# Two transformer blocks on one core: totals of the normalisations spread by products, first weights behind them unsplit, modulation in steps of eleven, mLSTM's gate projection among the scores

## The chip, the cores and the metric

The kernel runs on one core of one Trainium2 chip. The metric is the time of one execution in device microseconds (us). TensorE (PE) has two clocks, 1.2 and 2.4 GHz; the profile gives the granted clock of a stretch as a share of the full one. VectorE is DVE, ScalarE is ACT, GpSimd is POOL, and SP is the engine that issues most DMAs.

## What is computed

For 256 tokens of width 1024, in float32, a first block with two layers and a second block with two layers. Cut to what matters:

```python
h = layer_norm(x)
for l in range(2):                                   # first block
    cq, ckv, kr, xp, xqk, xv, xo, i, f = split(h @ w_in[l])
    mix = concat(mla(cq, ckv, kr), multiscale_pool(xp), mlstm(xqk, xv, xo, i, f)) @ w_out[l]
    h = layer_norm(ALPHA * h + mix)                  # ln1
    f = conv_glu_ffn(h, w_up[l], w_down[l])
    h = layer_norm(ALPHA * h + f)                    # ln2
for l in range(2):                                   # second block, c a vector of 1024
    sh1, sc1, g1, sh2, sc2, g2 = split(silu(c) @ w_ada[l] + b_ada[l])      # the modulation
    h = rmsnorm(x) * (1 + sc1) + sh1                 # rms0
    u, q, k, v = split(h @ w_in_2[l])
    y = concat(conformer_conv(u), band_attention(q, k, v)) @ w_out_2[l]    # conv with a layernorm, cln
    x = x + g1 * y
    h = rmsnorm(x) * (1 + sc2) + sh2                 # rms1
    x = x + g2 * (swiglu(h) if l == 0 else moe_top2(h))                    # 8 experts, router on h
```

## The kernel before

Everything is kept transposed: a tensor of 256 tokens by 1024 is eight tiles of 128 partitions (features) by 256 tokens. Weights come from HBM in chunks of about 1 MB, in one fixed order, into a ring of four slots (`ring`); SP's queue issues chunk n when chunk n-4 has been read. Most weights are used as a sum of two reduced-precision parts: ACT writes the high part of half a chunk (`whi`, L909), DVE the rest (`wlo`, L1301), four halves in turn, and the activations are split likewise into `HH` (ACT) and `HL` (DVE). A tile of a product is then three fast products (`mm3`: high by high, high by low, low by high). Small weights (`w_uq`, `w_uk`, `w_mqk`, `w_uv`) are used raw in float32, each product in two passes. `pair` makes two output tiles of one chunk, 48 fast products; `ahead(n)` splits the next chunk while the current one is used.

A **normalisation** (class `Norm`) subtracts a pilot (the mean of tile 0) from each tile into `XC`, squares it into `SQ` (ACT), and adds tiles up; POOL makes nearly all of these additions (L1861), DVE some. `norm_total` sends the added tiles, and the last `direct` ones singly, through PE against a column of 1/1024: the totals of 256 tokens arrive as two columns of 128 partitions. DVE makes mean and variance of these (2 elements a partition), ACT the root (L930, L934), DVE the reciprocal (L1352), and a `diagonal` (L1333) that a product with ones spreads over all partitions again. Then DVE centres (L1359) and scales (L1374), ACT applies gain and bias into `hT` (L941) and makes `HH`, DVE makes `HL` (L1382), tile by tile in turns, and the next `pair` takes each tile as its `HL` is done. There are eleven: ln0, ln1 and ln2 of two layers, rms0, cln and rms1 of two layers.

The **modulation** runs beside the first block as generators on SP, DVE, ACT and PE, advanced by `next(mod)` once after each chunk of `w_in` (but not w_in,5), `w_up` and `w_down`. A group has eight steps, each with one DVE operation on a 512 KB chunk of `w_ada` (L1415), then the split of the sum (ACT `acc_hi`, DVE `acc_lo` L1419), then PE's 16 small products and DVE's last addition. A group takes ten steps; PE's products stand one step behind `acc_lo`. SP has two buffers (`side`) and issues load n when the sum n-2 is made.

**mLSTM and attention of the first block.** After w_in,0 PE makes the score products of three units (32-row and 128-row operands), the q, k and pool products (`w_mqk`), and for each of four heads `selh` and `sc`; then `pair` of w_in,5 (the output gate), then `num`. ACT evicts the pool product (L971) behind the split of w_out,0.

Of the kernel before, what the change touches and what calls it, by code (L numbers as in the profile page):

```python
# [109 lines left out]
class Norm:  # L110


    def __init__(self, name, src, kt, about, weight, eps, ready, before, q=("POOL", "POOL"), direct=1, sq="ACT"):
        self.name, self.src, self.kt, self.about, self.weight, self.eps = name, src, kt, about, weight, eps
        self.ready, self.before, self.q, self.direct, self.sq = ready, before, q, direct, sq


def build(nc, t, dense=False):

    with ExitStack() as ctx:  # L120
# [36 lines left out]
        def over(name, at, *shape):  # L157
# [28 lines left out]
        g_pad, g_norm, g_mod, g_tap = (  # L186
            Signal(sem(n)) for n in ("pads", "norm_pool", "mod_pool", "taps_pool"))
# [7 lines left out]
                   g_norm, g_mod, g_tap, r_w, r_mm, r_hi, r_act, r_vec, d_w, d_mm, d_hi, d_act, d_vec,  # L195
# [46 lines left out]
        for l in range(DEPTH):  # L242
            for c in range(1, 5):
                chunk(("w_in", l, c), t["w_in"][l, c], (8, 256), "col")
# [11 lines left out]
            for j in range(NJ):  # L256
                chunk(("w_up", l, j), t["w_up"][l, j], (8, 256), "col")
# [3 lines left out]
        for l in range(DEPTH):  # L261
            for c in (0, 1, 2, 4, 5, 3, 6, 7, 8, 9):
                chunk(("w_in2", l, c), t["w_in2"][l, c], *(((8, 256), "col") if c < 4 else ((4, 512), "k")))
            for c in range(4):
                chunk(("w_out2", l, c), t["w_out2"][l, c], (8, 256), "col")
            if l == 0:
                for j in range(NJ):
                    chunk(("ffn_gu", j), t["ffn_gu"][j], (8, 256), "col")
# [3 lines left out]
        chunk(("w_router",), t["w_router"], (8, 8), "k")  # L272
        seq = [(e_, f) for e_ in range(NE) for f in range(NFB)]
        first_moe = len(chunks)
        for n in range(len(seq) + 1):
# [4 lines left out]
            if n > 0:  # L280
                for c in range(2):
                    chunk(("down", *seq[n - 1], c), t["moe_down"][seq[n - 1][0], seq[n - 1][1], c], (2, 1024), "k")

# [39 lines left out]
        def raw_read(n):  # L323
            if chunks[n][3] is None:
# [81 lines left out]
        N["ln0"] = Norm("ln0", xT, 8, True, C("i1024"), "eps5", x_in, None, ("DVE", "POOL"))  # L406
        N["ln1", 0] = Norm(("ln1", 0), xT, 8, True, C("i1024"), "eps5", after_out(0), "ln0", direct=2)
        N["ln2", 0] = Norm(("ln2", 0), xT, 8, True, C("i1024"), "eps5", after_down(0), ("ln1", 0))
        N["ln1", 1] = Norm(("ln1", 1), xT, 8, True, C("i1024"), "eps5", after_out(1), ("ln2", 0), direct=2)
        N["ln2", 1] = Norm(("ln2", 1), xT, 8, True, C("i1024"), "eps5", after_down(1), ("ln1", 1))  # L410
# [2135 lines left out]
```

## Time and profile before

| | |
|---|---|
| median of three runs | 2382.81 us (2377.18 to 2387.42) |
| the profiled execution | 2385.06 us, its span 2383.3 us |
| mean granted TensorE clock | 0.950 |
| busy share of the span | PE 94%, weight loads 81%, DVE 75%, ACT 59%, POOL 2% |
| chain that ended last | PE 70%, DVE 16%, ACT 11%, issue 2%, DMA 1% |
| HBM read | 571.75 MB, 240 GB/s over the span |

The first block takes 0 to some 755 us, the second block up to its router 1305 us, the experts the rest. Matmuls are pipelined, so a busy PE isn't PE at its peak: how far apart the starts of products lie tells more than the busy time. A bracket behind a row tells how long the engine was idle before it and what ended that.

### The profile page before, as it was taken

Reading aid. Unit: us, or ns where it says so; the run is one execution under the profiler, and the core shown is the slowest. Engines: PE = TensorE matmul, PEld = TensorE weight load, DVE = VectorE, ACT = ScalarE, POOL = GpSimd, SP = SyncE. Lnnn points to the kernel's source line nnn. Section 1 sums busy time; section 2 is a strip of 40 time slices with the busy share of each in tenths; the row PEclk is TensorE's granted clock in tenths of the full one; section 3 lists DMA queues with packets and bytes.
Section 4 is the critical chain, followed back from the end, with each engine's and each line's share of the span. In section 5 each row is a group of like instructions: output and inputs, shape, how many; then the busy total and the mean of one; then the engine's idle time right before and its main releaser. Section 6 shows DMA issues by size and latency. Waiting matters only on the chain.

```text
span 2383.3 us, 31840 instructions
## 1 busy us (share of the span) xinstructions
PE 2234.9 (94%) x12980; PEld 1936.8 (81%) x12980; DVE 1778.8 (75%) x2281; ACT 1407.8 (59%) x1977; POOL 53.3 (2%) x87
## 2 busy tenths in 40 slices
PE   6999998989997988999888999999999999999998
PEld 6789998879997878999877777777777777777776
DVE  5667876657876845665855888888888888888887
ACT  5445544445543745443745767676777777776775
POOL 0010000010001000000000000000000000000000
PEclk9789998889998998999997999999999999999999
DMA  5436665435666414766412788898888888898985
GB/s 209 144 107 223 234 219 192 139 131 195 232 212 219 151 36 151 248 218 224 174 49 106 294 321 343 313 349 338 337 335 330 341 322 348 324 358 310 348 337 193
DMA packets 89431, 574.92 MB, mean 241 GB/s; under 512 B 10048, under 2 KB 10176, under 8 KB 31040
## 3 DMA queue, kind: packets, MB, share of 16 engines
q1 hardware_dynamic: 87984, 566.89, 64.2%
q0 software_dynamic: 288, 3.15, 0.4%
q10 hardware_dynamic: 1008, 2.79, 0.3%
q8 instruction: 104, 1.70, 0.3%
q14 instruction: 47, 0.39, 0.0%
HBM read 571.75 MB, written 1.05 MB: 240 GB/s over the span
## 4 chain that ended last, share of the span: by engine, by line
PE 70%; DVE 16%; ACT 11%; issue 2%; DMA 1%; DVEq 0%; POOL 0%; ACTq 0%; POOLq 0%
PE bank L456 36%; PE bank L1964 33%; DVE wlo L1301 8%; ACT whi L909 4%; DVE side L1415 2%; ACT arena L2084 1%; ACT hsh L2089 1%; DVE arena L1646 1%; ACT hT L941 1%; DVE XC L1374 1%; DVE XC L1316 0%; ACT arena L1134 0%; DVE HL L1382 0%; ACT midh L1123 0%; DMA side<-in_w_ada 0%
## 5 line engine op out<-in xcount | busy, mean ns | idle before, releaser
L1301 DVE TENSOR_TENSOR wlo<-ring,whi 128x1024 fp32r<-128x1024 f32 (+1 forms) x1006 | 1150.2, 1191 | 161.8 <-ACT whi L909 151.7
L909 ACT ACTIVATE whi<-ring 128x1024 fp32r<-128x1024 f32 (+1 forms) x1006 | 992.5, 1026 | 199.1 <-PE bank L1964 145.2
L456 PE MATMUL bank<-HH,whi 128*128 128x256 f32 x1648 | 489.7, 297 | 39.9 <-DVE HL L1382 23.8
L456 PE MATMUL bank<-HH,wlo 128*128 128x256 f32 x1648 | 477.9, 290 | 0.0
L456 PE MATMUL bank<-HL,whi 128*128 128x256 f32 x1648 | 477.7, 290 | 0.0
L1964 PE MATMUL bank<-whi,xgh 128*128 128x512 f32 x896 | 365.9, 408 | 8.7 <-DVE wlo L1301 0.8
L456 PEld LDWEIGHTS bank<-HH,whi 128*128 128x128 f32 x1648 | 326.4, 198 | 55.8 <-issue 29.0
L1964 PE MATMUL bank<-whi,xgl 128*128 128x512 f32 x896 | 354.5, 396 | 0.0
L1964 PE MATMUL bank<-wlo,xgh 128*128 128x512 f32 x896 | 353.9, 395 | 0.0
L456 PEld LDWEIGHTS bank<-HL,whi 128*128 128x128 f32 x1648 | 328.0, 199 | 0.3
L456 PEld LDWEIGHTS bank<-HH,wlo 128*128 128x128 f32 x1648 | 327.2, 199 | 0.0
L1964 PEld LDWEIGHTS bank<-whi,xgh 128*128 128x128 f32 x896 | 168.3, 188 | 72.1 <-DVE wlo L1301 36.7
L1964 PEld LDWEIGHTS bank<-whi,xgl 128*128 128x128 f32 x896 | 167.9, 187 | 41.0
L1964 PEld LDWEIGHTS bank<-wlo,xgh 128*128 128x128 f32 x896 | 169.0, 189 | 35.2
L1964 PE MATMUL bank<-whi,hsh 128*128 128x512 f32 x448 | 181.1, 404 | 4.8 <-DVE wlo L1301 2.4
L1964 PE MATMUL bank<-whi,hsl 128*128 128x512 f32 x448 | 177.4, 396 | 0.0
L1964 PE MATMUL bank<-wlo,hsh 128*128 128x512 f32 x448 | 176.7, 394 | 0.0
L456 PE MATMUL bank<-midh,whi 128*128 128x256 f32 x528 | 153.9, 291 | 3.9 <-DVE wlo L1301 3.9
L456 PE MATMUL bank<-midl,whi 128*128 128x256 f32 x528 | 153.0, 290 | 0.0
L456 PE MATMUL bank<-midh,wlo 128*128 128x256 f32 x528 | 152.9, 289 | 0.0
L1415 DVE SCALAR_TENSOR_TENSOR side<-side,cact 128x1024 f32<-128x1024 f32 x84 | 107.4, 1279 | 2.9 <-DMA side<-in_w_ada 2.9
L1964 PEld LDWEIGHTS bank<-whi,hsh 128*128 128x128 f32 x448 | 84.1, 188 | 30.1 <-DVE wlo L1301 9.4
(265 smaller groups left out, 2530.0 us busy)
## 6 DMA issues: line engine op xcount, KB each, us to landing
ring<-in_moe_gate SPq DMA_DIRECT2D x112, 1024.0 KB, 6.3
ring<-in_moe_up SPq DMA_DIRECT2D x112, 1024.0 KB, 5.2
ring<-in_moe_down SPq DMA_DIRECT2D x112, 1024.0 KB, 5.3
side<-in_w_ada SPq DMA_DIRECT2D x96, 512.0 KB, 4.0
ring<-in_w_up SPq DMA_DIRECT2D x44, 1024.0 KB, 4.9
ring<-in_w_in SPq DMA_DIRECT2D x32, 1024.0 KB, 5.0
ring<-in_w_down SPq DMA_DIRECT2D x32, 704.0 KB, 4.3
ring<-in_ffn_gu SPq DMA_DIRECT2D x22, 1024.0 KB, 4.9
```

The lines of the kernel that those rows point to most:

```text
L456: return pe.matmul(out, lhsT, rhs, start=start, stop=stop, skip_group_check=True)
L909: a.activation(hi, part, ACT.Copy).then_inc(*made.up(("hi", n, i)))
L941: a.activation(dst[:, k, :], XC[:, k, :], ACT.Identity, bias=bias(k), scale=gain(k)).then_inc(*a_norm.up((s.name, "dst", k)))
L1301: v.tensor_tensor(lo, part, hi.bitcast(F32), ALU.subtract).then_inc(*done.up(("lo", n, i)))
L1374: v.tensor_tensor(XC[:, k, :], src[:, k, :], bc(r[:, 0:S], len(ks)), ALU.mult).then_inc(*v_norm.up(*((s.name, "nrm", x) for x in ks)))
L1415: v.scalar_tensor_tensor(side_acc, side_in[n % 2], cact[:, k:k + 1], side_acc, ALU.mult, ALU.add).then_inc(*v_mod.up(("acc", n)))
L1646: v.scalar_tensor_tensor(gc[:, s:S], b[:, S:512 - s], W(f"w_fconv{l}", (2 - s) * NJ + j), gc[:, s:S], ALU.mult, ALU.add).then_inc(*v_ffn.u ...
L1964: return pe.matmul(out, lhsT, rhs, start=start, stop=stop, skip_group_check=True)
L2084: a.activation(SGB[n % 2], PS[2 * (n % 2)][:, :], ACT.Silu).then_inc(*r_act.up(("silu", n)))
L2089: a.activation(flat(HSH[(n - 1) % 2][:, :, :]), PS[BANK["turn", n - 1]][:, :], ACT.Copy).then_inc(*r_hi.up(("hst", n - 1)))
```

## The change

Four parts; the diff is cut to its core.

1. **Totals.** All additions are DVE's (`norm_add`). PE multiplies the added tile and the `direct` last ones (2; for cln all 4, for rms0 of layer 0 all 8) as moving operand with a 128x128 matrix of 1/128 (`i128`), in float32: the total of each token arrives in every partition, 256 wide. ACT squares the mean and takes the root on 128x256, DVE makes the variance, centres all tiles, takes the reciprocal on 128x256, and scales. The diagonals and the two products with ones are gone. ACT makes all eight tiles of `hT` first, then `HH`; DVE makes `HL` (`low_parts`) after all scaling.
2. **Unsplit weights** (`WHOLE`): w_in,1, w_up,0, w_in2,0, ffn_gu,0 and the router's are used raw against `hT` in float32 (`pair_whole`), two products a tile k. `ahead` passes over them: the chunk after is split one turn earlier. Their slot is free when PE has read them.
3. **Modulation**: eleven steps a group, PE's products two steps behind `acc_lo`; two steps after each of w_in,1 to w_in,4, w_v and w_xp.
4. **The gate projection** (w_in,5) is cut into 16 tiles (`pair_by_tiles`), two after each head of score units 1 and 2, two after each head's `sc`. It is split before the convolution on DVE and before the eviction of w_in,0 on ACT; ACT evicts the pool product ahead of the exponentials of the heads.

```diff
@@ PE
+            def norm_finish(s, pause=lambda: None):
+                made[0] = s.name
+                banks = [take(s.name, "mean", until=[(v_norm, s.name, "cen", s.kt // 2 - 1)])] if s.about else [None]
+                banks.append(take(s.name, "sums", until=[(v_norm, s.name, "var")] if s.about else [(a_norm, s.name, "dev")]))
+                lim = s.kt - s.direct
+                tiles = ([None] if lim > 0 else []) + list(range(lim, s.kt))
...
+                for k in tiles:
+                    for i in range(2):
...
+                        tm = mm(banks[i][:, 0:S], C("i128"), src, k == tiles[0], k == tiles[-1])
+            def pair_whole(key, until):
...
+                for k in range(8):
+                    pe.wait_ge(*whole_h(k))
+                    for m in range(2):
+                        tm = mm(b[:, S * m:S * m + S], w[:, k, 128 * m:128 * m + 128], hT[:, k, :], k + m == 0, k == 7)
...
-                        for _ in range(9):
+                        for _ in range(10):
...
-                pair(("w_in", l, 1), src, [(a_proj, "cqs0", l)])
-                next(mod)
+                pair_whole(("w_in", l, 1), [(a_proj, "cqs0", l)])
+                for _ in range(2):
+                    next(mod)
...
+                gate = pair_by_tiles(("w_in", l, 5), src, [(a_proj, "xo", l)])
...
+                        for _ in range(2 if u else 0):
+                            next(gate)
...
-                pair(("w_in", l, 5), src, [(a_proj, "xo", l)])
+                    for _ in range(2):
+                        next(gate)
+                next(gate, None)
@@ ACT
-                if n + 1 < first_moe and chunks[n + 1][3] is not None:
-                    split(n + 1)
+                m = n + 1 + (n + 1 in WHOLE)
+                if n not in WHOLE and m < first_moe and chunks[m][3] is not None:
+                    split(m)
...
+                split(CH["w_in", l, 5])
                 a.wait_ge(*p_w("w_in", l, 0, 1))
...
+                b = PS[BANK["pool", l]]
+                a.wait_ge(*p_mla("pool", l))
+                for m in range(2):
+                    proj(("pool", l, m), RAW[:, 4 + m, :], b[:, S * m:S * m + S], scale=W(f"s_pool{l}", m))
                 for h in range(4):
@@ DVE
+                if s.about and 0 < k < lim:
+                    norm_add(s, 0, k)
+                if 1 < k <= lim and k - 1 < lim:
+                    norm_add(s, 1, k - 1)
...
+                    for j in range(len(js)):
+                        centred(j)
+                v.wait_ge(*a_norm(s.name, "dev"))
+                v.reciprocal(RSTD[:, 0, :], RSTD[:, 0, :]).then_inc(*v_norm.up((s.name, "rstd")))
...
+                split(CH["w_in", l, 5])
                 v.wait_ge(*a_proj("xqk", l))
@@ SP
-                        yield
-                        if n > 8:
+                        for _ in range(3 if n > 8 else 1):
                             yield
...
-                return key[0] in ("w_v", "w_xp") or key[0] == "w_in" and key[2] != 1
+                if key[0] == "w_in":
+                    return (0, 0, 2, 2, 2, 1)[key[2]] if key[2] else 2
+                return 2 if key[0] in ("w_v", "w_xp") else 0
```

## Rows read from the trace of the kernel before

**Rows 1.** The page, busy us of each engine (share of the span).
```profile
PE 2234.9 (94%) x12980; PEld 1936.8 (81%) x12980; DVE 1778.8 (75%) x2281; ACT 1407.8 (59%) x1977; POOL 53.3 (2%) x87
```

**Rows 2.** Waits of PE: for whom, us in total, times, longest us.
```profile
PE bank L456 <- DVE HL L1382: 27.5, 26, 2.2
PE bank L456 <- DVE acc_lo L1419: 13.4, 5, 5.3
...
PE bank L456 <- DVE RSTD L1333: 10.6, 9, 1.7
PE bank L456 <- ACT XC L971: 7.9, 2, 4.0
PE bank L456 <- POOL RSTD L1861: 7.9, 1, 7.9
```

**Rows 3.** Stretches: length, busy PE, PEld, DVE, ACT, POOL; granted clock, DMA share, GB/s.
```profile
161.00:180.00 19.00, 14.36 (x70) 12.07 (x71) 12.35 (x25) 10.00 (x18) 0.00 (x0) 0.64 0.22 69
...
310.00:326.00 16.00, 10.71 (x61) 10.54 (x60) 7.22 (x11) 5.60 (x9) 0.00 (x0) 0.68 0.50 165
```

**Rows 4.** Timeline around ln1 of layer 0: start us, us, engine, line, operation.
```profile
157.38 2.89 DVE L1301 TENSOR_TENSOR wlo<-ring,whi 128x1024 fp32r<-128x1024 f32 x2 [1.43 <-ACT whi L909]
...
160.98 0.42 DVE L1625 SCALAR_TENSOR_TENSOR xT<-hT,bank 128x256 f32<-128x256 f32 x1
...
165.02 1.28 DVE L1359 TENSOR_TENSOR XC<-XC,bank 128x512 f32<-128x512 f32 x2
...
168.58 0.55 PE L456 MATMUL bank<-HH,whi 128*128 128x256 f32 x1 [2.15 <-DVE HL L1382]
...
180.39 0.28 PE L456 MATMUL bank<-HH,whi 128*128 128x256 f32 x1
```

**Rows 5.** Reciprocals on DVE by shape: count, busy us, mean ns, idle before.
```profile
L1352 DVE RECIPROCAL small<-small 128x2 f32<-128x2 f32 x11 | 1.8, 166 | 11.1 <-ACT small L934 7.2 <-ACT small L930 3.9
...
L1725 DVE RECIPROCAL arena<-arena 128x16 f32<-128x16 f32 x4 | 1.0, 252 | 14.9 <-ACT arena L1191 14.9
```

**Rows 6.** Timeline, raw float32 passes of 256 columns, at either clock.
```profile
71.66 5.56 PE L456 MATMUL bank<-arena,ring 128*128 128x256 f32 x25
...
99.82 3.78 PE L456 MATMUL bank<-arena,ring 128*128 128x256 f32 x8
```

**Rows 7.** Timeline of PE at rms0 of layer 0 and at the router.
```profile
767.58 0.99 PE L456 MATMUL bank<-cst,RSTD 128*128 128x1 f32 x4 [7.86 <-POOL RSTD L1861]
...
1292.10 0.35 PE L456 MATMUL bank<-whi,HH 128*128 128x8 f32 x1 [2.21 <-DVE HL L1382]
...
1304.57 3.67 PE L882 MATMUL bank<-cst,hT 128*128 128x128 f32 x16
```

**Rows 8.** Timeline from the scores of layer 0 to `num`, PE and DVE.
```profile
82.77 17.12 PE L456 MATMUL bank<-arena 128*128 128x128 f32 x48
...
105.66 0.42 DVE L1574 TENSOR_TENSOR SQ<-bank,cst 128x256 f32<-128x256 f32 x1 [3.33 <-PE bank L456]
...
116.50 1.65 PE L456 MATMUL bank<-arena 64*128 64x256 f32 x4 [3.96 <-ACT XC L971]
118.08 0.58 PE L456 MATMUL bank<-HH,whi 128*128 128x256 f32 x1
...
125.00 2.79 PE L456 MATMUL bank<-arena,SQ 128*128 128x65 f32 x24
```

**Rows 9.** Stretches within it, columns as in rows 3.
```profile
92.00:97.00 5.00, 5.00 (x11) 2.67 (x11) 4.63 (x9) 2.37 (x11) 0.00 (x0) 0.50 0.00 0
...
104.00:108.00 4.00, 4.00 (x14) 2.62 (x15) 2.31 (x7) 2.14 (x9) 0.00 (x0) 0.87 0.52 141
```

**Rows 10.** Timeline of DVE at the start of w_down of layer 0.
```profile
314.51 1.69 DVE L1301 TENSOR_TENSOR wlo<-ring,whi 128x768 fp32r<-128x768 f32 x2 [0.31 <-ACT whi L909]
316.12 1.22 DVE L1419 TENSOR_TENSOR acc_lo<-side,acc_hi 128x1024 fp32r<-128x1024 f32 x1
```

**Rows 11.** DMA issues of the first 140 us: count, KB each, median us to landing.
```profile
side<-in_w_ada SPq DMA_DIRECT2D x8, 512.0 KB, 6.0
```

More of the change, by code:

```diff
@@ L405, in build @@
         N = {}
[L406 to L410, printed above, removed]
@@ L416, in build @@
-        N["cln", 1] = Norm(("cln", 1), CA, 4, True, C("i512"), "eps6", lambda k: conv_made(1, k), ("rms0", 1), ("DVE", "DVE"))
-        N["rms1", 1] = Norm(("rms1", 1), xT, 8, False, C("i1024"), "eps6", lambda k: v_res("out2", 1, k), ("cln", 1), direct=2)
+        N["ln0"] = Norm("ln0", xT, 8, True, "eps5", x_in, None)
+        N["ln1", 0] = Norm(("ln1", 0), xT, 8, True, "eps5", after_out(0), "ln0")
+        N["ln2", 0] = Norm(("ln2", 0), xT, 8, True, "eps5", after_down(0), ("ln1", 0))
+        N["ln1", 1] = Norm(("ln1", 1), xT, 8, True, "eps5", after_out(1), ("ln2", 0))
@@ new lines, in build @@
+        N["ln2", 1] = Norm(("ln2", 1), xT, 8, True, "eps5", after_down(1), ("ln1", 1))
+        N["rms0", 0] = Norm(("rms0", 0), xT, 8, False, "eps6", lambda k: a_norm(("ln2", 1), "dst", k), ("ln2", 1), direct=8,
+                            sq="DVE")
+        N["cln", 0] = Norm(("cln", 0), CA, 4, True, "eps6", lambda k: conv_made(0, k), ("rms0", 0), direct=4)
+        N["rms1", 0] = Norm(("rms1", 0), xT, 8, False, "eps6", lambda k: v_res("out2", 0, k), ("cln", 0))
+        N["rms0", 1] = Norm(("rms0", 1), xT, 8, False, "eps6", lambda k: v_res("down2", k), ("rms1", 0))
@@ L419, in conv_made @@
+        N["cln", 1] = Norm(("cln", 1), CA, 4, True, "eps6", lambda k: conv_made(1, k), ("rms0", 1), direct=4)
+        N["rms1", 1] = Norm(("rms1", 1), xT, 8, False, "eps6", lambda k: v_res("out2", 1, k), ("cln", 1))
         def conv_made(l, m):
@@ L931, in norm_dev @@
                 else:
[L932 to L936 removed]
+                    a.wait_ge(*p_norm(s.name, "sums"))
+                    a.activation(RSTD[:, 0, :], b[:, 0:S], ACT.Sqrt, bias=C(s.eps), scale=1.0 / s.kt).then_inc(
+                        *a_norm.up((s.name, "dev")))
@@ L981, in act_program @@
                 norm_tile(N["ln0"], k)
-            split(0)
+            split(CH["w_in", 0, 2])
             norm_dev(N["ln0"])
@@ L986, in act_program @@
             for l in range(DEPTH):
-                split(CH["w_in", l, 2])
                 b = PS[BANK["w_in", l, 1]]
@@ L1046, in act_program @@
                 next(mod)
-                split(CH["w_in", l, 5])
                 a.wait_ge(*v_lstm("conv", l))
@@ L1558, in dve_program @@
                 next(mod)
-                split(CH["w_in", l, 5])
                 ends, causal = [], C("causal")
@@ L1661, in dve_program @@
                         norm_tile(N["ln2", l], k)
-                norm_finish(N["ln2", l], affine(N["ln2", l], hT, then=N["rms0", 0] if l else None))
+                norm_finish(N["ln2", l])
+                if l == 0:
+                    low_parts(N["ln2", 0])
+                else:
+                    for k in range(8):
+                        norm_tile(N["rms0", 0], k)
             def rms_modulated(which, l):
@@ L1932, in sp_program @@
                     next(mod)
-                if NSLOT <= n < first_moe and stepped(chunks[n - NSLOT][0]):
+                for _ in range(steps_behind(chunks[n - NSLOT][0]) if NSLOT <= n < first_moe else 0):
                     next(mod)
```

355 lines of the change are left out of this document (159 added, 196 removed).

## The prediction, made before the changed kernel was run

> **What bounds the kernel now.** I read the page's shares first, then who makes PE wait, then PE's clock by stretches, then the timelines of the places named there. PE is busy 94% of the span [rows 1], and behind a loaded weight the products follow at an even pitch (about 0.12 us a fast product in w_out,3 and in the pair that ends at 180.39), so time comes off only where PE waits, where its clock is down, or where it does fewer passes. The list of waits [rows 2] gives the places: `HL` in the normalisations 27.5 us, `acc_lo` 13.4, the diagonals (`RSTD`) 10.6, ACT's eviction of the pool product 7.9, POOL's additions 7.9 once. Each wait costs again behind itself: over the 19 us around ln1 PE is idle 4.6 and the granted clock is 0.64; over 16 us around an `acc_lo` wait it is idle 5.3 at 0.68 [rows 3]. Full clock is 2.4 GHz, 0.50 is 1.2 GHz. Behind the router's stage nothing changes, so all that is won stands at the router's end and stays.
>
> **Totals and unsplit weights.** From the last tile of xT at 160.98 to the first product behind the first pair at 180.39 ln1 takes 19.4 us [rows 4]: PE gets its first `HL` at 168.6, does 48 passes, most of them at half clock. The new chain, from that start a: 0.9 us to the last square, products with `i128` to a+2.0, variance a+2.5, four centrings at 0.61 apiece (the two in rows 4 took 1.28) to a+4.95, a reciprocal on 128x256, one scaling (0.42) and one tile of `hT` (0.5). The reciprocal isn't in the trace at this size. Its rows [rows 5] are 166 ns at 2 elements, 252 at 16: 6.1 ns an element, so 1.7 us at 256. The near bound is the pace of the simple operations (0.4 us), the far one that the slope grows by half (2.3). I take 1.7, the slope being the only row. That gives a+7.7 for the first tile, against a+7.6 before: the start doesn't move. What moves is the pair: 32 raw passes instead of 48. A raw pass is 5.56/25 = 0.222 us at full clock, 3.78/8 = 0.47 at half [rows 6]; 48 fast passes are 5.7 and 10.2. With about 5 us at half clock (11 passes) and 21 at full I get 9.6 us, range 8.8 to 10.5, so the pair ends at a+17.3: 2.1 gained. DVE's new additions in w_out are ten of 0.43 = 4.3 us; they lie in DVE's idle of 1.43 before each `wlo` [rows 4] for three of four chunks, and the last 1.0 is paid. ln1 gains 1.1 in each layer. By the same steps: ln0 2.6 (no additions on the path, PE starts on the weights at 22), ln2 of layer 0 1.5, rms1 of layer 0 and rms0 of layer 1 1.7 each, cln nothing (no pair behind it, its time is in the scores' shade). At rms0 of layer 0 POOL's 7.9 go [rows 7] and the column products of 3.7 behind it too; eight full products at half clock (7.4) and two longer reciprocals (3.0) come, and the diagonals' 1.5 go: 2.7. Sum 12.4.
>
> The Trainium skill ("VectorE: DVE Perf Modes", First, the fixed hardware budget) speaks against this part: the reciprocal is an iterative divide repeated eight times on the same slices. If an element then cost eight times that of an addition (0.42/256 = 1.6 ns, with its fixed part off about 1.0), an estimate by that page is some 2.2 us, and with nine such reciprocals on the path 5 us of the gain would be gone. The sum above goes by the slope of the rows.
>
> **Router.** Before, its first product starts at 1292.10 and its last pass ends at 1304.57: 48 narrow passes of 0.21 with two `HL` waits [rows 7]. Raw it is 32 passes at the same pitch, 6.9 us. The last square ends near 1287.0; total, root 0.45, reciprocal 1.7, scaling 0.45, `hT` 0.5 give a start at 1290.8 and an end at 1297.7: 6.9 gained. Both parts together 19.3.
>
> **Modulation.** With products two steps behind `acc_lo`, the five waits (13.4) should go where DVE was merely late, and with them the half clock behind them: in rows 3 10.7 us of busy PE at a mean of 0.68. Over the five I count 13.6 us lost to the clock. At 312 something stays: `wlo` and `midl` would be 2.3 of the 5.3 late even without `acc_lo` (the DVE rows around 316.1 show `wlo` behind `acc_lo`'s 1.22 [rows 10]). Saved: about 17 of 27. New cost: steps now come twice a chunk in the projections. A load of 512 KB takes 6.0 us to land [rows 11] and DVE's step 1.28, against 5.7 us for a pair, with two loads in it; so DVE falls behind by about 1 us a chunk there and the first group's products, now at w_xp of layer 0, wait some 2.8 us for `acc_lo`, plus the clock behind (1.7) and half a us of a late split: -5. SP's queue: two buffers, a load waits for the sum two before, and the ring's loads stand behind it; the ring has four slots in hand, so they aren't late by that much. DVE's steps in the gated and down stages are as before, one a chunk, and the number of steps, 122 before and 134 after, is met by the doubling. Net 12.
>
> **Gate projection among the scores.** In layer 0, T0 = 82.77 is the start of the scores, `num` starts at T0+42.2 [rows 8]. From 87 to 103 the clock is 0.50 [rows 9]: 32-row products of the scores leave it there, DVE and ACT pace them (DVE 5.0 of 5 us from 87, 4.6 of 5 from 92). The heads take 104.93 to 118.08 = 13.2 us with 3.96 of eviction wait, then the pair 6.9. After: 16 tiles of a third of a us to 0.64 each at either clock are put in; eight in the scores, eight in the heads. The eviction wait goes (pool product ahead of the exponentials), the heads become DVE-bound (0.42+0.28+0.56 and ACT between) at 2.15 to 2.3 a head, 9.2 in all, and contain eight tiles. In the scores, eight tiles at half clock are 5.1 us of PE; half of it lies in PE's waits for DVE, the rest lengthens them. The splits of w_in,5 (DVE 2.35, ACT 1.04) are now ahead of convolution and eviction, those of w_out,0 behind: 1.4 lost. Likeliest the scores stay at half clock: gain 13.2+6.9-9.2 = 10.9, less 3.5, less 1.4 = 6 a layer, 12 in two. If the added products lift the clock, the scores' 17 us shrink by some 8: 14 a layer. The bad end is near nothing, 0.3.
>
> **Sum.** 19.3 + 12 + 12 = 43 off the profiled execution of 2385.06 (span 2383.3, 1.8 outside) is 2342; that execution lies 2.3 above the median, so against the median of 2382.81 it is **2340**.
>
> **Rivals.** (a) The clock stays up through the scores in one layer or both: for it, full-array products between the 32-row ones; against it, DVE and ACT pace that stage at 4.6 to 5.0 of 5 us. One layer 2331, both 2323, and with the raw pairs lifted sooner 2318. (b) DVE or the side loads become the bound in the doubled stages: two 512 KB loads in a pair of 5.7 us, landing 6.0 plus 1.28. If each chunk is late by 1.6, twelve chunks cost 19, and with the added additions only 18 of the gain is left: 2365. For it, the 6.0 [rows 11]; against it, that the median is over the crowded first 140 us. (c) The other side: raw float32 pairs don't lift the clock. Then each of eight runs at 0.46 throughout, 14.4 instead of 9.8 (37 us), and the pair behind it starts cold (8 x 1.7 = 14): 51 lost against 43 gained, 2390. It decides from the point where a raw pair ends below 0.75 of the clock. Against it: the granted clock rose to 0.87 right behind the eight raw products from 99.82, beginning within them [rows 6, 9]. (d) The change does little of what it says because each wait is replaced by one as long (the centrings, now all ahead of the first scaling, push the tile as far as `HL` did, and w_xp takes over `acc_lo`'s 13.4): 2378.
>
> **How the numbers follow.** Likeliest case 0.45; (a) 0.30; (b) 0.16; (c) 0.04; (d) 0.05. The range holds the likeliest with its unknown costs (reciprocal ±5, the scores ±6) and reaches into (a) down to both layers with something to spare, and to (b): 2315 to 2366. About 0.5% (12 us) is what a measurement of this kernel can tell from no change. Faster by more than that are the first three but for an edge of (b): 0.90; within it (d) and that edge: 0.06; slower: 0.04.
>
> **What would show it.** RECIPROCAL 128x256 at 1.7 us on DVE; no addition on POOL; PE's first raw pass 7.7 us after the start of the last xT of ln1, then 32 passes at 0.46 falling to 0.22, end at a+17.3; `acc_lo` under 4 us in all, most of it once, at w_xp of layer 0; no wait for L971's successor before the last head, and `num` at T0+36; granted clock in the scores 0.50; the router's last pass 6.9 us after its first. Wrong would be: a raw pair at half clock to its end; a reciprocal over 2.3; idle of PE before w_v, w_xp or w_in,0 put down to `wlo`; the scores' span above 25 us with no gain in the heads.

## The result and the profile after

The changed kernel takes 2363.16 us (median of six, 2357.26 to 2370.51) against 2383.57 (six runs, 2377.18 to 2387.42): ratio 0.992, 95% interval 0.9904 to 0.9937. I had forecast 2340, a gain of 43 us; 20 came. The profiled execution of the changed kernel took 2358.97 us, its span is 2357.2. Against the profiled execution of before that is 26 us less; the 6 beside the medians' 20 are where the two executions lie among the runs of their kernels. The stages below are read from these two traces, so they add up to 26.

From the page of the changed kernel: the busy line of the engines, which stands beside [rows 1], and DVE's reciprocals at their new size, beside [rows 5] (columns as there).

```profile
PE 2218.2 (94%) x12766; PEld 1917.4 (81%) x12766; DVE 1784.1 (76%) x2276; ACT 1393.6 (59%) x1960; POOL 2.2 (0%) x17
...
L1411 DVE RECIPROCAL RSTD<-RSTD 128x256 f32<-128x256 f32 x11 | 19.2, 1748 | 9.8 <-ACT RSTD L982 9.6
```

PE is busy 16.7 us less, POOL does none of the additions. Waits of PE in the changed kernel (for whom, us in total, times, longest), beside [rows 2]:

```profile
PE bank L458 <- ACT hT L989: 39.5, 8, 6.2
PE bank L458 <- DVE wlo L1349: 16.6, 11, 2.7
...
PE bank L458 <- DVE SQ L1380: 7.6, 1, 7.6
PE bank L458 <- DVE HL L1461: 7.2, 7, 2.8
...
PE bank L458 <- DVE XC L1377: 6.0, 4, 2.0
PE bank L458 <- DVE RSTD L1369: 5.9, 1, 5.9
...
PE bank L458 <- DVE acc_lo L1446: 1.9, 1, 1.9
```

`HL` 27.5, `RSTD` 10.6 and POOL 7.9 of before are `hT` 39.5 and `SQ` 7.6 now: the normalisations still make PE wait as long, in one piece each. The wait for `SQ` is the new form of POOL's 7.9: at rms0 of layer 0 PE waits until DVE has squared the tiles. `acc_lo` fell from 13.4 to 1.9 and ACT's eviction of the pool product is gone. So the waits went much as the change says. The stages say where the time went instead. Each boundary is the start or the end of a PE product of the timeline that is named in the first column; the last column is the prediction's term.

| stage (us) | before | after | difference | forecast |
|---|---|---|---|---|
| to the end of ln0's first pair | 36.5 | 34.2 | -2.3 | -2.6 |
| projections, from there to the scores, layers 0 and 1 | 46.3, 46.3 | 54.5, 53.7 | +15.6 | +5 |
| scores to the first head | 22.2, 20.6 | 24.9, 24.9 | +7.0 | +7 |
| heads and the gate's pair | 20.1, 20.1 | 10.3, 10.3 | -19.5 | -21.8 |
| `num` and w_uv | 6.1, 6.1 | 12.6, 12.7 | +13.1 | +2.8 |
| attention to w_out's end | 29.6, 29.6 | 29.6, 29.6 | 0.0 | 0 |
| ln1, ln2, ln2 with rms0, rms1, rms0 of layer 1, cln | | | -9.3 | -9.8 |
| router | 19.3 | 12.4 | -6.9 | -6.9 |
| up and down, three times | 207.1, 205.5, 201.4 | 200.4, 198.9, 190.8 | -23.9 | -17 |
| experts and the rest | 1078.7 | 1078.8 | +0.1 | 0 |

The sum is -26.1, the difference of the two spans. Two terms failed: `num` and w_uv by 10.3, the projections by 10.6. The heads gave 2.3 less than forecast and the up and down stages 6.9 more; with about 1 us of the small terms that is the 17 between 43 and 26. One group of modulation products in each layer now stands in the projections and not in the up and down stages: some 4 of the +15.6 and of the -23.9 have only moved. Timeline of PE in the changed kernel, from the last head to w_uv, and under it the same products in the stretches (columns as in [rows 3]); [rows 8] has `num` of before:

```profile
120.77 0.69 PE L458 MATMUL bank<-xT,cst 4*128 4x256 f32 x2
...
123.97 1.80 PE L458 MATMUL bank<-arena,SQ 128*128 128x65 f32 x8
127.23 3.67 PE L458 MATMUL bank<-arena,SQ 128*128 128x65 f32 x16 [1.45 <-ACT arena L1013]
130.70 6.06 PE L458 MATMUL bank<-ring,arena 128*128 128x512 f32 x8
```

```profile
114.00:122.00 8.00, 8.00 (x41) 5.71 (x40) 4.75 (x13) 3.27 (x10) 0.00 (x0) 0.99 0.88 328
122.00:124.00 2.00, 2.00 (x10) 1.78 (x9) 0.94 (x3) 2.00 (x4) 0.00 (x0) 0.50 0.00 0
124.00:130.00 6.00, 4.55 (x22) 4.36 (x22) 2.77 (x4) 3.21 (x6) 0.00 (x0) 0.50 0.00 0
130.00:136.00 6.00, 6.00 (x12) 3.01 (x12) 2.68 (x7) 0.77 (x2) 0.00 (x0) 0.54 0.00 0
```

The heads run at 0.99 of the clock; from 122 it is 0.50 until 136. Before, 24 products of `num` took 2.79 us and eight of w_uv 3.65, both behind a pair in one piece, and the clock, which was down in the heads, was up again (kernel before, columns as above):

```profile
108.00:120.00 12.00, 8.04 (x24) 5.57 (x23) 4.34 (x10) 5.01 (x10) 0.00 (x0) 0.50 0.45 173
121.00:131.00 10.00, 10.00 (x68) 8.16 (x67) 3.45 (x10) 3.37 (x7) 0.00 (x0) 1.00 0.00 0
```

So the tail, `num` and w_uv, grew by 6.5 us in two ways: PE stands idle for 1.45 in the middle of `num`, where it never waited before, and the products themselves take 5 us longer at half clock.

### The profile page after: what moved, and what is told of

Same layout as the page of the kernel before. It is cut to its first block, busy times and chain, and to the rows that moved or that the text cites. A ratio compares the mean times of both kernels' runs of the same rounds, so it can differ in the third digit from the quotient of the medians.

```text
span 2357.2 us, 31258 instructions
## 1 busy us (share of the span) xinstructions
PE 2218.2 (94%) x12766; PEld 1917.4 (81%) x12766; DVE 1784.1 (76%) x2276; ACT 1393.6 (59%) x1960; POOL 2.2 (0%) x17
## 3 DMA queue, kind: packets, MB, share of 16 engines
q10 hardware_dynamic: 1008, 2.79, 0.3%
## 4 chain that ended last, share of the span: by engine, by line
PE 71%; DVE 15%; ACT 10%; issue 2%; DMA 1%; SPq 0%; DVEq 0%; ACTq 0%
PE bank L458 37%; PE bank L1973 34%; DVE wlo L1349 8%; ACT whi L954 4%; DVE side L1442 2%; ACT arena L2093 1%; ACT hsh L2098 1%; DVE arena L1681 1%; DVE RSTD L1411 1%; DMA ring<-in_w_in 1%; DVE XC L1399 1%; ACT arena L1181 0%; DMA side<-in_w_ada 0%; ACT midh L1170 0%; DVE XC L1377 0%
## 5 line engine op out<-in xcount | busy, mean ns | idle before, releaser
L1349 DVE TENSOR_TENSOR wlo<-ring,whi 128x1024 fp32r<-128x1024 f32 (+1 forms) x990 | 1128.5, 1187 | 116.2 <-ACT whi L954 106.0
L954 ACT ACTIVATE whi<-ring 128x1024 fp32r<-128x1024 f32 (+1 forms) x990 | 978.0, 1028 | 179.0 <-PE bank L1973 145.2
L458 PE MATMUL bank<-HH,whi 128*128 128x256 f32 x1536 | 447.0, 291 | 18.5 <-DVE wlo L1349 11.1
L458 PE MATMUL bank<-HH,wlo 128*128 128x256 f32 x1536 | 439.1, 286 | 0.0
L458 PE MATMUL bank<-HL,whi 128*128 128x256 f32 x1536 | 438.4, 285 | 0.0
L458 PEld LDWEIGHTS bank<-HH,whi 128*128 128x128 f32 x1536 | 297.3, 194 | 28.2 <-issue 16.9
L458 PEld LDWEIGHTS bank<-HL,whi 128*128 128x128 f32 x1536 | 297.9, 194 | 0.5
L458 PEld LDWEIGHTS bank<-HH,wlo 128*128 128x128 f32 x1536 | 297.8, 194 | 0.0
```

Source lines behind the costliest of these rows:

```text
L458: return pe.matmul(out, lhsT, rhs, start=start, stop=stop, skip_group_check=True)
L954: a.activation(hi, part, ACT.Copy).then_inc(*made.up(("hi", n, i)))
L1349: v.tensor_tensor(lo, part, hi.bitcast(F32), ALU.subtract).then_inc(*done.up(("lo", n, i)))
```

## The experiments

Stages are named as in the table. "Tail" is `num` and w_uv. e1 to e6, e8 and e9 were run once, e7 and e10 to e12 four times; since the six runs of the changed kernel spread over 13 us, the single runs are read by their stages.

**e1.** Is it the pair's place that costs the tail its clock?

```diff
-                        for _ in range(2 if u else 0):
-                            next(gate)
...
-                    for _ in range(2):
-                        next(gate)
-                next(gate, None)
+                for _ in gate:
+                    pass
```

> From the changed kernel, the output gate's pair (w_in,5) stands again in one piece behind the four heads; its split, the pool product's early eviction and all else stay. Measured by stages: from the start of the scores to the end of the w_uv products took 47.9 us in both layers of the changed kernel (24.9 to the first head, 10.3 heads, 12.6 num and w_uv) and 48.4 and 46.9 before. Theory (the pair behind the heads was what lifted the clock for num and w_uv, 6.1 us at full and 12.6 at half clock): 22.2 + 9.6 + 6.9 + 6.1 = 44.8, so 3.1 a layer less, kernel about 2357. Rival (num and w_uv are slow because of what ACT and DVE do beside them, not because of the clock): 22.2 + 9.6 + 6.9 + 12.6 = 51.3, kernel about 2370.

Measured: 2343.9. Layer 0: scores 20.6, heads and pair 14.7, tail 6.1, in all 41.4; layer 1: 14.2, 16.3, 6.1, in all 36.6; in the changed kernel 47.9 in both. The two lines of the tail in e1 and the stretches around it:

```profile
123.45 2.79 PE L458 MATMUL bank<-arena,SQ 128*128 128x65 f32 x24
126.08 3.65 PE L458 MATMUL bank<-ring,arena 128*128 128x512 f32 x8
```

```profile
114.00:120.00 6.00, 6.00 (x25) 5.59 (x26) 4.00 (x6) 3.08 (x6) 0.00 (x0) 0.50 0.52 212
120.00:124.00 4.00, 4.00 (x34) 4.00 (x33) 0.00 (x0) 0.34 (x2) 0.00 (x0) 0.93 0.00 0
124.00:130.00 6.00, 6.00 (x33) 4.04 (x32) 3.44 (x9) 3.25 (x8) 0.00 (x0) 1.00 0.00 0
```

PE comes out of the heads at half clock here too, but 48 full products without a break stand behind them, and the clock is back before `num`. The tail takes 6.1, as the theory said. The edit took away two things at once, though: the tiles, and the wait of 1.45 in the middle of `num`. So it shows that the tail's 6.5 us come from where the gate stands; it doesn't show how they divide between the clock and the wait (see e2 and e8). The whole is better than the theory's 44.8, since the scores of layer 1 ran at full clock and took 14.2. The heads without tiles take 6.6 us (108.75 to 115.36), not the 9.2 that I had put down as DVE's pace.

**e2.** All tiles among the heads, none in the scores (the first edit of e1, and `range(4)` for `range(2)` in the heads).

> From the changed kernel, all 16 tiles of the gate stand among the heads, four behind each, none in the scores. Theory of the clock: 12 full products a head (1.4 us at full clock) beside 1.6 of the head's own hold the clock up, so scores 22.2, heads 4 x 3.1 = 12.4, num and w_uv 6.1: 40.7 against 47.9, kernel about 2349. Rival: the heads' 64-row products and the waits for DVE keep the clock down or let it fall again; heads 4 x 4.8 = 19 and the tail 12.6: 54, kernel about 2375.

Measured: 2350.91. Heads with all tiles 12.3 and 12.6, as the theory had it (12.4); scores 20.6 and 14.2; but the tail 12.0 and 12.1, as the rival. So neither as a whole. Four tiles a head do cost only their own time, and they do hold the clock up: the first eight products of `num` take 1.00, the full clock's time, where they took 1.80 in the changed kernel. Then PE waits, and only with that wait does the clock fall:

```profile
121.10 1.00 PE L458 MATMUL bank<-arena,SQ 128*128 128x65 f32 x8
124.58 3.67 PE L458 MATMUL bank<-arena,SQ 128*128 128x65 f32 x16 [2.47 <-ACT arena L1011]
128.05 5.18 PE L458 MATMUL bank<-ring,arena 128*128 128x512 f32 x8
```

```profile
109.00:121.00 12.00, 12.00 (x72) 9.56 (x72) 5.43 (x14) 5.11 (x16) 0.00 (x0) 1.00 0.61 220
124.00:131.00 7.00, 6.42 (x20) 4.87 (x21) 2.46 (x8) 0.76 (x3) 0.00 (x0) 0.52 0.00 0
```

That wait of 2.47 (1.45 in the changed kernel) is for ACT's sigmoid eviction of the gate's bank, and it is the kernel's own doing. `take` hands out the eight banks, the buffers that products are written to, in turn. With the tiles the gate's bank is taken early and held to the last tile, and by the order of the turns the second half of `num` gets that very bank, so it must wait until ACT has emptied it. With the pair behind the heads the gate's bank is taken last and `num` gets the two that follow: in e1 the eviction ends 2.8 us behind the start of `num`, when `num` is through, and no product has waited for it. How long the wait lasts is ACT's order: behind the last exponential it does the split of w_out,0 (1.99), the high parts (0.70) and a table load (1.28) before the eviction.

**e3.** The modulation alone goes back (ten steps, one a chunk, products one step behind).

```diff
-                        for _ in range(3 if n > 8 else 1):
+                        for _ in range(2 if n > 8 else 1):
...
-                        for _ in range(10):
+                        for _ in range(9):
                             yield
                         b = take("mod", l, g, until=[(v_mod, "mod", l, g)])
...
-                for _ in range(2):
-                    next(mod)
+                next(mod)
```

> From the changed kernel, the modulation goes by ten steps again, one a chunk, PE's products one step behind acc_lo. Theory (the doubled steps made DVE late in the projections): from the end of the first raw pair to the scores 54.5 -> 47 us in layer 0 and 53.7 -> 46.5 in layer 1; the up and down stages 200.4, 198.9 and 190.7 -> 207, 205.5 and 201; kernel 8 us slower. Rival (the projections are late for DVE's low parts behind the normalisation and the raw pair's half clock, not for the steps): both stay over 52, and the kernel is 24 us slower.

Measured: 2373.89. Projections 46.5 and 46.5; up and down 206.9, 202.8 and 200.0. So the modulation made 15.3 of the projections' 15.6 and 19.6 of the 23.9 in the up and down stages; its net worth in the changed kernel is 4.3, where 12 was forecast. The low parts behind the normalisation and the raw pair cost the projections next to nothing; the other 4.3 of the up and down stages came with them or with the freed ring slots, which wasn't tried apart. The kernel is 15 us slower than the profiled changed kernel and not 8. The rest lies in layer 1, from the scores to the tail's end (52.3 for 47.9), in ln1 (21.2 for 19.0) and in ln2 with rms0 (32.1 for 28.7), which this edit doesn't touch.

**What delays the projections.** The changed kernel, layer 1, DVE and PE behind w_in,3 (timeline):

```profile
412.73 2.68 DVE L1442 SCALAR_TENSOR_TENSOR side<-side,cact 128x1024 f32<-128x1024 f32 x2 [4.37 <-DMA side<-in_w_ada]
417.48 2.36 DVE L1349 TENSOR_TENSOR wlo<-ring,whi 128x1024 fp32r<-128x1024 f32 x2 [2.07 <-ACT whi L954]
...
418.85 0.55 PE L458 MATMUL bank<-HH,whi 128*128 128x256 f32 x1 [2.28 <-DVE wlo L1349]
```

```profile
415.45 1.06 ACT L1006 ACTIVATE acc_hi<-side 128x1024 fp32r<-128x1024 f32 x1 [4.86 <-DVE side L1442]
416.41 1.99 ACT L954 ACTIVATE whi<-ring 128x1024 fp32r<-128x1024 f32 x2
```

DVE waits 4.4 us for a side load (SP issued it and its neighbour at 404.8, right behind two ring loads at 403.9 and 404.3), makes two sums; only then can ACT split the accumulator, and the split of the next weights stands behind that on ACT's queue, DVE's `wlo` behind that, and PE's pair last: 2.28 us of idle PE, and half clock for parts of the two pairs behind. In layer 0 the chain is another: DVE waits for side loads 2.0 us in all there, and the late one for PE is `acc_lo` (1.9), the wait that I had priced. Over the whole stage (columns as in [rows 3], changed kernel, layers 0 and 1):

```profile
34.00:88.70 54.70, 52.21 (x363) 49.26 (x362) 38.68 (x56) 25.09 (x38) 0.00 (x0) 0.94 0.62 217
...
403.50:457.30 53.80, 51.52 (x363) 49.81 (x363) 33.53 (x49) 21.77 (x35) 0.00 (x0) 0.94 0.60 212
```

PE is idle 2.5 and 2.3 us of it (not at all before); the clock's mean is 0.94 (1.00 before), which at 54 us is 3 us; the 16 products of a modulation group (363 for 347 in this stage of layer 0) take 2.5 and 1.7, and before the change they stood elsewhere. DVE is busy 38.7 of 54.7 us: its mean load is no bound. That the doubled steps make the 15 us is borne out by every version that was run: with them the stage takes 50.8 to 54.7 us (the changed kernel, e1, e2, e4, e5, e9), without them 46.3 to 46.5 (e3, e6 to e8, e10 to e12). The chain through the late load is read from one place of one trace.

**e6.** Distance without doubled steps: e1, with groups of ten and one step a chunk, and PE's products two steps behind `acc_lo`, because the next group's first sum takes the step in which DVE added the bias.

```diff
+                yield
                 yield
                 for l in range(DEPTH):
                     for g in range(6):
-                        for _ in range(10):
+                        for _ in range(9):
                             yield
                         b = take("mod", l, g, until=[(v_mod, "mod", l, g)])
...
+                            if k == 0 and n > 0:
+                                add(*divmod(6 * l + g - 1, 6))
```

> From e1 (gate pair behind the heads): groups of ten steps, one step a chunk everywhere as before the change, but PE's products stay two steps behind acc_lo: the next group's first sum takes the step of DVE's last addition. Theory (the gain in the up and down stages comes from the distance alone, the loss in the projections from the doubled steps alone): projections 46.5 in both layers (54.7 and 53.6 in e1), up and down stages 200.4, 201 and 191 as in e1, so 15 us less than e1, about 2330. Rival (the gain came from the longer groups, that is fewer sums per chunk): the up and down stages go back toward 205, and the kernel is within 5 us of e1.

Measured: projections 46.5 and 46.5; up and down 200.0, 197.7, 193.4, together 591.1 against 590.1 in the changed kernel. The stages are what the theory said: the gain in the up and down stages is the distance's, the loss in the projections the doubling's. The time is 2341.77, though, only 2 less than e1, not 15: of the 15.2 that the projections gave, 11.6 went in the scores, which took 22.2 and 24.2 at half clock where e1 had 20.6 and 14.2, and 1.6 in the heads and pair of layer 0. The stretches of layer 1's scores in e1 and of layer 0's in e12, the same kernel as e6:

```profile
458.00:466.00 8.00, 8.00 (x34) 5.23 (x34) 7.63 (x16) 5.01 (x16) 0.00 (x0) 1.00 0.01 2
```

```profile
84.00:101.00 17.00, 17.00 (x38) 10.09 (x36) 13.43 (x26) 5.14 (x15) 0.00 (x0) 0.50 0.00 0
```

**e8.** Half of the gate among the heads, the other eight tiles in a row behind them, modulation as in e6.

> From the changed kernel, no gate tile in the scores, two behind each head, the other eight in one row behind the heads. Modulation as in e6. Theory of the clock: the eight in a row lift it for num and w_uv as the whole pair did: heads 10.0, the row 4.0, num and w_uv 6.1, together 20.1 against 20.8 to 22.4 in e1. Rival: eight don't lift it, and num and w_uv take 12 us again, 26 in all.

Measured: 2348.62; heads and row 12.3 and 13.8, tail 11.5 and 9.9: 23.8 and 23.7. The sum is nearer to the rival's (26), but its reason is not what happened. The clock was up when `num` began, in both layers: its first eight products took 1.00. Then PE waited 1.88 for the gate's bank, and the clock fell behind that, in layer 0 at once, in layer 1 in the products of w_uv. Layer 0:

```profile
115.21 1.00 PE L458 MATMUL bank<-arena,SQ 128*128 128x65 f32 x8
118.10 3.32 PE L458 MATMUL bank<-arena,SQ 128*128 128x65 f32 x16 [1.88 <-ACT arena L1007]
```

```profile
103.00:116.00 13.00, 13.00 (x81) 10.56 (x80) 7.92 (x17) 6.83 (x18) 0.00 (x0) 1.00 0.53 203
118.50:125.00 6.50, 6.50 (x20) 4.43 (x20) 2.67 (x7) 0.20 (x2) 0.00 (x0) 0.50 0.00 0
```

In layer 1 the clock was down as the row began and up again before `num`. So the row of eight does what the theory wanted, as far as the start of `num`.

All tails together: the pair stands in one piece in seven of the kernels (before, e1, e6, e7, e10 to e12), and their fourteen tails take 6.1 us each, without a wait. With tiles there are fourteen too, 9.9 to 13.7 us, and in each PE waits for the gate's bank, 1.1 to 3.2 us. In seven of them (both layers of e2 and e8, layer 0 of e3 and e9, layer 1 of e4) `num` begins at full clock and the clock falls during the wait or behind it. In the other seven, both layers of the changed kernel among them, the clock is at 0.50 already when `num` begins. There the wait can't have brought it down; whether it keeps it down isn't shown. Tiles with another bank for `num` are the run that is missing: it would say whether the gate can be cut up for free. Of what was tried, one piece behind the heads (e1 and e6: 20.8 to 22.4 for heads and tail) is the best place.

**e4.** The normalisations: PE's totals waited 2.0 us for the last `XC`, since their bank was the pilot's.

```diff
-                if s.about and k == s.kt - 1:
-                    held.discard(BANK[s.name, "pilot"])
...
+                if s.about:
+                    held.discard(BANK[s.name, "pilot"])
                 lim = s.kt - s.direct
```

> From the changed kernel, PE's pilot bank stays held until the two banks of the totals have been taken, so the totals don't wait for the last XC. Theory (the products of the added tiles wait 2.0 us at ln1, and at ln2 1.0, for a bank that the last subtraction frees): the first raw pass comes 10.8 - 1.5 = 9.3 us after PE's last w_out product, kernel about 5 us less. Rival (the last square and its products set the start anyway, at 168.5 of ln1): 10.8 stays within 0.5.

Measured: 2360.76; ln1 18.2 and 18.4 against 19.0 and 19.0, ln2 of layer 0 17.6 against 18.0. From the last product of w_out (168.1) to the first raw pass (177.5) it is 9.4 us in layer 0, 10.7 in the changed kernel: the theory's cause and nearly its size (1.5). The kernel's time, 2.4 under the median of the changed kernel, can't be told from no change. What is late next is DVE's last addition, 0.72:

```profile
167.93 0.60 PE L458 MATMUL bank<-RSTD,cst 128*128 128x256 f32 x2
169.24 0.70 PE L458 MATMUL bank<-RSTD,cst 128*128 128x256 f32 x2 [0.72 <-DVE RSTD L1369]
```

**e5.** Reciprocal ahead of the centrings, then centre and scale two tiles at a time.

```diff
-                    for j in range(len(js)):
-                        centred(j)
                 v.wait_ge(*a_norm(s.name, "dev"))
...
                     if s.about:
+                        centred(j)
                         v.wait_ge(*v_norm(s.name, "cen", j))
```

> From the changed kernel, DVE takes the reciprocal before the centrings, and then centres and scales two tiles at a time. Theory (the centrings, 2.4 us, stand ahead of the first scaling, and only the first pair of tiles is needed for PE to start): the first raw pass of ln1 comes 3 x 0.61 = 1.8 us sooner, 10.8 -> 9.0 us behind PE's last w_out product, and the end of the pair by 1.0 to 1.8; five normalisations with a mean, kernel 5 to 8 us less. Rival (the tiles then come at DVE's 0.62 us each pair half and the raw passes wait, or the clock stays down longer): end of the pair unchanged within 0.5.

Measured: 2363.09; ln1 19.0 and 18.5, ln2 of layer 0 17.8, but ln2 of layer 1 with rms0 32.6 against 28.7. In the timeline of ln1 PE waited 4.75 for the first `hT` where it had waited 5.81, and yet the first pass came no sooner behind the last product of w_out, 10.9 against 10.7, since the totals ran partly at half clock:

```profile
168.49 1.01 PE L458 MATMUL bank<-SQ,cst 128*128 128x256 f32 x2
169.29 1.06 PE L458 MATMUL bank<-XC,cst 128*128 128x256 f32 x2
170.14 1.06 PE L458 MATMUL bank<-SQ,cst 128*128 128x256 f32 x2
175.96 2.47 PE L458 MATMUL bank<-hT,ring 128*128 128x256 f32 x5 [4.75 <-ACT hT L989]
```

The same passes took 0.59 for two in the changed kernel. In layer 1 of e5 they did too, and there the first pass comes 9.7 us behind the last product of w_out, 1.0 sooner and not 1.8, and the pair ends 0.5 sooner. By the end of the pair the rival holds in both layers. In front of rms0 all eight tiles are wanted, not the first: there the order costs 3.9.

**e7.** Both, on e6.

> e6 with e4's held pilot bank and e5's order of reciprocal and centring. If the parts add up: 2330 - 5 - 3 = 2322. If the interleaving isn't worth anything behind the earlier totals: 2330.

Measured: 2340.82 (2332.06 to 2343.67), ratio 0.9822 (0.9792 to 0.9852). ln1 16.7 and 17.2, ln2 of layer 0 16.8 (18.5 to 20.9 in e6); ln2 of layer 1 with rms0 31.6 (27.7 in e6), the convolution stage of layer 1 134.5 (132.8). ln0 and these three normalisations gained 9.1 on e6; ln2 with rms0 and the convolution stage gave back 5.6, the up and down stages 3.4.

**e9.** What the raw pair is worth: w_up,0 of layer 0 split again.

```diff
-        WHOLE = {CH["w_in", l, 1] for l in range(DEPTH)} | {CH["w_up", l, 0] for l in range(DEPTH)}
+        WHOLE = {CH["w_in", l, 1] for l in range(DEPTH)} | {CH["w_up", 1, 0]}
```

> From the changed kernel, w_up,0 of layer 0 alone is split again (48 fast passes behind HL), layer 1 keeps its raw pair: the two are compared within one run. Theory (the raw pair is worth the time that PE no longer waits for HH and HL): the totals and the start of hT as now, but HL of the first two tiles comes after all eight hT and the first HH, 4.0 + 0.5 + 0.6 us later; from PE's last w_out product to the end of the first pair 19.0 -> 24 in layer 0, 19.0 in layer 1. Rival (the clock gives it back, since 48 fast passes load PE more): below 21 in layer 0.

Measured: 2356.69; from PE's last product of w_out to the end of the first pair 25.2 in layer 0 and 20.9 in layer 1 (19.0 in the changed kernel; the totals of this run were partly at half clock in both layers). The raw pair is worth 4.3 between the two layers of this run, near the theory's 5 (6.2 against the changed kernel, the clock included), and the rival's bound of 21 is out. This holds in the new order alone, where `HL` comes behind all eight `hT`: in the kernel before, tile by tile in turns, ln1 with a split pair took 19.6 and 19.7, only 0.7 more than with the raw pair now. The split pair waits 10.48 for `HL` (5.80 for `hT`, the raw pair, in layer 1):

```profile
181.88 0.55 PE L458 MATMUL bank<-HH,whi 128*128 128x256 f32 x1 [10.48 <-DVE HL L1424]
```

**e10.** From the kernel before, two edits alone: the pool product's eviction ahead of the exponentials, and e6's distance.

```diff
+                b = PS[BANK["pool", l]]
+                a.wait_ge(*p_mla("pool", l))
+                for m in range(2):
+                    proj(("pool", l, m), RAW[:, 4 + m, :], b[:, S * m:S * m + S], scale=W(f"s_pool{l}", m))
                 for h in range(4):
                     a.wait_ge(*v_lstm("ex0", l, h))
```

> From the kernel before, two small edits only: ACT evicts the pool product ahead of the heads' exponentials, and PE's modulation products come two steps behind acc_lo in groups of ten, as in e6; normalisations, weights and the gate's pair are as before. Theory: up and down stages 207.1, 203.8 and 201.4 -> 200.4, 199 and 193 (21 us), the heads 2 x 3.96 less (8 us), projections unchanged at 46.3: 2383 - 29 = 2354, that is as much as the whole change gave. Rival (the normalisations carried the change): above 2370.

Measured: 2352.48 (2349.24 to 2355.83), ratio 0.9874 (0.9855 to 0.9893): ahead of the changed kernel's 0.992 (0.9904 to 0.9937), without any of its normalisations. Projections 46.3, up and down 199.9, 199.9 and 193.3, heads and pair 13.2 and 16.4 against 20.1. (The 203.8 in the expectation should be the table's 205.5.) Its list of waits has neither `acc_lo` nor the eviction, and the normalisations' waits nearly unchanged beside [rows 2]:

```profile
PE bank L456 <- DVE HL L1383: 27.5, 26, 2.2
PE bank L456 <- DVE wlo L1302: 14.6, 13, 3.3
...
PE bank L456 <- DVE RSTD L1334: 11.1, 9, 1.7
PE bank L456 <- POOL RSTD L1867: 7.9, 1, 7.9
```

**e11 and e12.** e11 is e6 with the held bank, and with reciprocal first only where the first tiles are wanted first; e12 is e6 timed beside it.

```diff
+            def early(s):
+                return s.about and s.kt == 8 and s.name != ("ln2", 1)
```

> e6 with the held pilot bank and with reciprocal first in ln0, ln1 and ln2 of layer 0 only (behind ln2 of layer 1 all tiles are squared again, and the interleaving made that stage 3.9 us longer in e5 and e7). If the stages add up: 2 us less than e6 at each of four normalisations, 8 us; kernel 2333. If the half clock takes it back: within 3 us of e12.

> e6 timed beside e11 and e10, for their comparison: 2342 if the one look was typical; if the scores of layer 1 run at full clock as in e1, 2332.

Measured: e11 2331.53 (2329.46 to 2332.76), ratio 0.9784 (0.9768 to 0.98); e12 2341.78 (2338.16 to 2342.62), ratio 0.9829 (0.9812 to 0.9845). Both intervals are apart, so e11 is the best version: 51 us under the kernel before and 32 under the changed one. It is also 21 us under e10, the two small edits alone; that is about what the normalisations and the router gave in the changed kernel (18.5). In the two traces ln1 of layer 0, ln2 of layer 0 and ln1 of layer 1 take 16.8, 17.6 and 16.8 against 21.0, 18.4 and 20.9; part of those is the clock in e12's totals, as in e5. At ln2 of layer 1 with rms0 e11 stays 2.2 behind (29.9 against 27.7); that is not explained.

## Why the prediction was wrong

**The normalisations and the router** were right as a sum, -18.5 for -19.3, and the sum is partly luck: ln1 gained 0.7 in each layer for 1.1, ln2 of layer 0 0.9 for 1.5, rms1 and rms0 of layer 1 2.7 each for 1.7, and the convolution stages with cln, put at nothing, lost 1.2. The router gave its 6.9. The mechanism stood, with the reciprocal at 1.75 us where the slope of [rows 5] gave 1.7. The Trainium skill's iterative divide ("VectorE: DVE Perf Modes", First, the fixed hardware budget) made an estimate of 2.2 of it; the row says 1.75, so eight times an addition is too much here. (Two slips in the working changed nothing: its steps add up to a+7.6, not a+7.7, and a slope half as large again gives 2.5, not 2.3.) Inside ln1 two errors met: the first raw pass came 9.7 us behind the start of the last xT, not 7.7 (the totals waited for the pilot's bank and are twelve passes one behind the other), and the raw pair then took 8.3, not 9.6.

**The clock in the raw pairs.** Rival (c) is out: the pair of ln1 runs its 32 passes from 176.87 to 185.5 at a mean of 0.27, between the 0.47 and 0.222 of [rows 6], and the pair that follows takes 0.12 a pass.

**The modulation's stages** were right in sign and low in size: 23.9 for 17. I had left 2.3 of the 5.3 at 312 and more to `wlo` and `midl`; in the changed kernel the idle time at that place is 2.17, for `wlo`. The second block gave 10.6 of the 23.9, and the clock of this stage went from a mean of 0.97 to 1.00.

**The projections** are the first failed step. I had reckoned DVE late by a little each chunk and priced one late `acc_lo`, 2.8, and its clock, 1.7, in layer 0 alone. The stage lost 15.6 in both layers, and e3 and e6 show that it goes with the doubled steps: 4.8 of it is idle PE, 4.2 the products of the two groups that moved here, the rest, 6.6, the clock. Layer 0 went as I had said (one late `acc_lo`, 1.9), but the clock cost about 3 there and the moved products 2.5, which my sum didn't have. Layer 1, which I had put at nothing, lost 7.4, and in it acted what I had named as rival (b): a side load landed too late for two a pair. By its size (b) fits, 1.3 for each of twelve chunks where I gave it 1.6, but it wasn't a little at each chunk: PE waited at two places in layer 0 (1.9 and 0.6) and at one in layer 1 (2.3). What I took as "against" was the median of the load times over 140 us; the one load that counts was issued behind two ring loads, and DVE waited 4.4 for it. What I didn't see at all is its path: ACT's split of the accumulator stands ahead of its split of the weights.

**The tail of the gate** is the second. My sum had the scores +3.5 a layer (measured 2.8 and 4.3), the heads with their pair -10.9 (measured -9.7 and -9.8), and 1.4 for what ACT and DVE do later; the last is the tail's 6.5 and 6.6. I had counted the pair of w_in,5 as 6.9 us to be hidden, and asked neither what stands behind it nor which bank it holds. [rows 8] show `num` at 0.11 us a product right behind the pair, and the clock before the pair was 0.50. In the changed kernel `num` and w_uv run at half clock, 5 us more, and PE waits 1.45 and 1.50 for the gate's bank. e1 gives all of it back, and is 6.5 and 11.3 us a layer shorter: the tail by 6.5 and 6.6, the scores by 4.3 and 10.7 (in layer 1 at full clock), while the heads with the pair are 4.4 and 6.0 longer. From the scores to the tail's end the changed kernel gained 0.5 in layer 0 and lost 1.0 in layer 1, with the early eviction in it, which alone gave 6.8 and 3.7 us in e10. So moving the gate into the scores and heads cost time.

**The other rivals.** (a), the clock through the scores, didn't come in the changed kernel, where the tiles lengthened them at half clock; it came in layer 1 of e1 and e2, which have none there, and in layer 1 of e9, which has the tiles as in the changed kernel (17.0 us at a mean of 1.00). So the tiles don't decide it. (d) is out by the normalisations. The time of 2363 lies at what (b) would give, 2365, but that is chance: (b) was at most half of what was missing.

## What to carry to other kernels

Before a block of dense products is cut up and spread into waits, look at what runs behind it and at what it holds while it lasts. Here the products behind the block need 6.1 us where it stands in one piece and 9.9 to 13.7 where it is cut up: the clock was down as they began, or it fell with the wait for the bank that the cut block had held. Doubling the rate of a background stream isn't free merely because the engines' mean load leaves room: count the loads that must land within one chunk, what is issued ahead of them, and what stands behind the waiting step on each queue. A longer distance between a producer and its consumer could be had here by overlapping groups instead of stretching them (e6), and two small edits found by the list of waits (e10) beat a large one that mixes gains and losses.

## What the runs showed of the hardware

- The stage from the scores to the first head, with the same products in the same order and no tiles among them, took 22.2 and 20.6 us before, 20.6 and 14.2 in e1, 22.2 and 24.2 in e6, 22.2 and 22.3 in e8. With the tiles of the changed kernel it took 24.9 twice there and 26.5 and 17.0 in e9. The spread goes with the granted clock (1.00 in layer 1 of e1 and of e9, 0.50 in [rows 9] and in e12). Why it holds in one and not in another with the same work isn't settled, and it is as large as most of the effects sought here: a kernel's time alone, from one run, tells them apart badly, its stages well.
- The clock was lost with short waits: in layer 0 of e2 and e8 PE went idle at full clock for 2.47 and 1.88 us, and the products behind ran at 0.52 and 0.50 (stretches there); the tails took 12.0 and 11.5 us for 6.1.
- Two raw float32 passes of 256 columns against a 128x128 matrix take 0.59 us at full and 1.06 at half clock (busy as modelled), so even the totals of ln1 depend on the clock: 2.8 us from the first to the last in the changed kernel, 4.1 in e5.
- A reciprocal on 128x256 takes 1.75 us, 1748 ns over eleven, four times an addition of that size (0.42).
